# Second block's input projection in seven half-size products, with the gates ahead of attention and the conv projection inside it

## The reference, cut to what matters

```
h   = modulate(rmsnorm(x, norm1_g), shift, scale)            # 1024 x 1024
q, k, v, u, gate_b, gate_c, g_attn, g_conv = split(h @ w_in)  # 1024, 256, 256, 5 x 1024 columns
q, k = axial rope(q), axial rope(k)                           # x * cos + rotate_half(x) * sin
o  = window attention(q, k, v, k_ctx, v_ctx, sink)            # 16 heads, 4 kv heads, +-128 keys + 256 context keys
z  = gate_c * u
y  = gate_b * (w0 * z[t-1] + w1 * z[t] + w2 * z[t+1])         # short conv along the tokens
m  = sigmoid(g_attn) * (o @ w_proj_attn) + sigmoid(g_conv) * (y @ w_proj_conv)
x  = x + mod * (m @ w_out)
```

## Time and profile before

| what | value |
|---|---|
| median of 3 runs | 2936.88 us (2932.27 to 2942.73) |
| the profiled execution | 2934.08 us, its span 2932.3 us |
| PE busy | 96% of the span, DVE 62%, ACT 45%, POOL 18% |
| second block's modulation and first products | about 1165 to 1232 us of the span |
| q and conv groups | to 1581 us |
| attention with the gates | 1582 to 2010 us |
| the two projections | 2011 to 2188 us |

### The profile page before, as it was taken

The page is one execution under the profiler, slowest core; times in us unless marked ns, Lnnn a source line. Parts: engine busy times, 40 slices in busy tenths (PEclk is TensorE's granted clock), DMA queues, the critical chain, the costliest instruction groups (busy, mean ns, idle before and its releaser), DMA issues.

```text
span 2932.3 us, 34943 instructions
## 1 busy us (share of the span) xinstructions
PE 2803.8 (96%) x13928; PEld 2237.2 (76%) x13928; DVE 1827.3 (62%) x2535; ACT 1332.1 (45%) x1927; POOL 527.8 (18%) x437
## 2 busy tenths in 40 slices
PE   8999999999999999999999999999999399999996
PEld 6777777888778778888887666667888378888885
DVE  5344535888875778643223555554445679999997
ACT  4344433333333454211113666664223267777775
POOL 0001202555554011330000111111000300000000
PEclk9999999999999999999999999999999699999998
DMA  4110132445653993411211111115324579999996
GB/s 155 40 44 30 44 108 80 122 134 149 185 151 134 346 265 115 130 44 55 75 51 40 44 41 43 36 41 170 112 92 163 227 282 391 395 398 398 397 394 236
DMA packets 256550, 465.79 MB, mean 159 GB/s; under 512 B 28860, under 2 KB 135508, under 8 KB 255876
## 3 DMA queue, kind: packets, MB, share of 16 engines
q1 hardware_dynamic: 229648, 377.00, 36.8%
q0 software_dynamic: 26592, 86.51, 9.3%
q10 hardware_dynamic: 148, 0.04, 0.0%
HBM read 409.92 MB, written 53.58 MB: 158 GB/s over the span
## 4 chain that ended last, share of the span: by engine, by line
PE 89%; DVE 5%; DMA 2%; ACT 2%; issue 1%; SPq 0%; POOL 0%; POOLq 0%; DVEq 0%; ACTq 0%
PE PS L129 83%; PE PS L132 6%; DVE m L138 2%; DMA m<-in_w_down_dram 1%; ACT m L135 1%; DVE m L144 1%; DVE m L180 0%; DVE m L183 0%; ACT L135 0%; DVE m L177 0%; SPq L186 0%; DMA m<-h_scratch 0%; DVE m L147 0%; DMA m<-in_x_dram 0%; DMA m<-xh_scratch,small 0%
## 5 line engine op out<-in xcount | busy, mean ns | idle before, releaser
L129 PE MATMUL PS<-m,m 128*128 128x512 f32 (+5 forms) x12118 | 2622.8, 389 | 35.2 <-DVE m L138 20.9
L129 PEld LDWEIGHTS PS<-m,m 128*128 128x128 f32 (+2 forms) x12118 | 2034.3, 184 | 548.2 <-issue 115.6
L135 ACT ACTIVATE m<-m 128x512 fp32r<-128x512 f32 (+5 forms) x722 | 735.7, 1040 | 815.0 <-PE PS L129 422.6
L138 DVE TENSOR_TENSOR m<-m,m 128x512 fp32r<-128x512 f32 (+7 forms) x713 | 911.3, 1308 | 251.1 <-ACT m L135 211.7
L135 ACT ACTIVATE m<-PS 128x512 f32<-128x512 f32 (+3 forms) x499 | 280.9, 583 | 497.5 <-PE PS L129 334.4
L138 DVE TENSOR_TENSOR m<-PS,m 128x512 fp32r<-128x512 f32 (+1 forms) x356 | 232.8, 684 | 331.8 <-PE PS L129 297.7
L138 POOL TENSOR_TENSOR m<-m,m 128x512 f32<-128x512 f32 (+3 forms) x166 | 265.0, 1599 | 563.8 <-DVE small L147 207.9
L132 PE MATMUL PS<-ident,m 128*128 128x128 f32 x1586 | 222.9, 280 | 69.1 <-DVE m L153 36.0
L132 PEld LDWEIGHTS PS<-ident,m 128*128 128x128 f32 x1586 | 193.5, 145 | 103.9 <-DVE m L153 36.3
L135 ACT ACTIVATE m<-m,small 128x640 f32<-128x640 f32 (+4 forms) x200 | 157.4, 789 | 220.5 <-DVE small L141 155.0
L147 DVE CUSTOM_DVE_ANT_0 m<-PS,m 128x640 f32<-128x640 f32 (+4 forms) x192 | 146.4, 775 | 118.4 <-PE PS L129 118.4
(11 more groups left out here) (87 smaller groups left out, 489.8 us busy)
## 6 DMA issues: line engine op xcount, KB each, us to landing
m<-in_w_exp_gate_dram SPq DMA_DIRECT2D x64, 1024.0 KB, 8.8
m<-in_w_exp_up_dram SPq DMA_DIRECT2D x64, 1024.0 KB, 9.0
m<-in_w_exp_down_dram SPq DMA_DIRECT2D x64, 1024.0 KB, 8.4
m<-in_w_mod_dram SPq DMA_DIRECT2D x48, 512.0 KB, 3.7
m<-in_w_gate_up_dram SPq DMA_DIRECT2D x44, 512.0 KB, 6.5
m<-in_w_in_dram SPq DMA_DIRECT2D x41, 512.0 KB, 4.1
m<-in_w_in_dram SPq DMA_DIRECT2D x12, 1024.0 KB, 5.2
h_scratch<-m POOLq DMA_DIRECT2D x22, 512.0 KB, 3.5
```

Source lines behind the costliest of these rows:

```text
L129: return Unsent() if self.e is None else self.e.matmul(o, l, r, start=first, stop=last, **k)
L135: return Unsent() if self.e is None else self.e.activation(o, i, fn, **k)
L138: return Unsent() if self.e is None else self.e.tensor_tensor(o, a, b, op)
```

## The change: what it does

- k, q, gate_b/u/gate_c and both gates (25 slabs of 256 weight columns, `ST`) are made by seven half-size products each, ahead of attention, in one loop over c = 0 to 24. v and the context's k, v stay as they were.
- The modulated x2 is kept in place (x2 is stored to DRAM first, tile by tile), and four block differences T1 to T4 are turned and split beside the four plain blocks.
- Rope works on the four quarters of each slab in three buffers, and its results go to DRAM (`q_scratch`); q and k are loaded back before attention.
- The final norm's product on the x2 residual moves from eight instructions in a row to two a pass in four gate passes, with a load and a store of each tile.
- In attention the filler is the conv projection, 16 groups (6 matmuls a step, from step 3 on, three parts after the last step), ended by a product with the loaded gate on DVE (`pc_take`) and a store. The first six steps also split y. The sigmoids and their loads of activation tables leave attention.
- The proj stage has 16 groups in place of 32.

```
+        ST = [("k", 0)] + [("q", c) for c in range(4)] + [
+            p for j in range(4) for p in (("b", j), ("u", 2 * j), ("u", 2 * j + 1))] + [("g", j) for j in range(8)]
+        ST_ORDER = "P1 P6 P2 P7 P5 P4 P3".split()
+        def st_first(act, c):
+            act.wait_ge("st_acc", c, "P1")
+            if c:
+                act.wait_ge("st_up", c - 1, "12")
+            act.activation(su2, ps("st_acc", c, "P1"), ACT.Copy)
...
+        def second_pe(pe):   # the end of it
+            st_product(pe, 0, "P1"), (pe, 0, "P2"), (pe, 0, "P5")
+            4 turns of T2; P7; 4 turns of T4; P6, P4, P3
+            for c in range(1, NST):
+                for P in ST_ORDER:
+                    st_product(pe, c, P)
...
+        def second_dve(dve):  # its loop
+            for c in range(NST):
+                if c == C_AT["b", 0]:
+                    dve.wait_ge("rope_st0", 18)
+                    dve.memset(zb, 0.0)
+                st_u2(dve, c)
+                rope_join(dve, 4 * c - 1)
+                st_low(dve, c + 1, "P1"); st_low(dve, c + 1, "P6")
+                # taps 0 and 1 of the conv tile of pass c - 1, if any
+                st_low(dve, c + 1, "P2")
+                # gate passes 1 to 4: two tiles of residual_norm
+                st_u3(dve, c)
+                rope_turn(dve, 4 * c)
+                # taps 2 and 3
+                st_low(dve, c + 1, "P7")
+                st_c22(dve, c)
+                rope_join(dve, 4 * c); rope_turn(dve, 4 * c + 1)
+                st_low(dve, c + 1, "P5")
+                st_c21(dve, c)
+                rope_join(dve, 4 * c + 1); rope_turn(dve, 4 * c + 2)
+                st_low(dve, c + 1, "P4")
+                st_c12(dve, c)
+                rope_turn(dve, 4 * c + 3); rope_join(dve, 4 * c + 2)
+                st_low(dve, c + 1, "P3")
...
+        def second_pool(pool):  # its loop
+            for c in range(NST):
+                st_sums(pool, c + 1)
+                rope_pool(4 * c - 1); rope_store(4 * c - 2)      # while there is rope
+                rope_pool(4 * c);     rope_store(4 * c - 1)
+                rope_pool(4 * c + 1); rope_store(4 * c)
+                rope_pool(4 * c + 2); rope_store(4 * c + 1)
+                # conv_store, zb_gate (gate_c * u), gate_store, residual_store in their passes
...
+        def rope_join(dve, n):
+            dve.wait_ge("rope_cos", n)
+            dve.wait_ge("rope_sin", n)
+            dve.tensor_tensor(a, a, b_, ALU.add)
...
-                if s == 0:
-                    gate_part(pe, s, 0, 4)
                 if s + 1 < NS2:
                     qk2(pe, s + 1)
-                if s > 1:
-                    gate_part(pe, s, 0, 2)
+                fill_part(pe, s - FILL0, 0)
                 turn2(pe, s, 0)
                 turn2(pe, s, 1)
-                if s > 1:
-                    gate_part(pe, s, 2, 1)
+                fill_part(pe, s - FILL0, 1)
                 if len(chunks2(s)) == 3:
                     turn2(pe, s, 2)
...
+        def mix_dve(dve):   # its first steps
+            for s in range(NS2):
+                if s == 0:
+                    w_low(dve, W_PC)
+                    w_low(dve, W_PC + 1)
                 if s + 1 < NS2:
                     max2(dve, s + 1)
                 p2_evacuate(dve, s, 1)
                 p2_evacuate(dve, s, 2)
+                for h, k in y_parts(s):      # 4 in steps 0 and 1, 2 in steps 2 to 5
+                    y_low(dve, h, k)
...
         def proj_dve(dve):
+            dve.wait_ge("pc_st0")
+            dve.wait_ge("pc_st1")
```

More of the change, by code:

```diff
@@ L332, in program @@
                 pair(w2, 1536 + mt * 128, 3584 + mt * 128)
-        W_G = len(WT)
-        for j in range(16):
-            feat(w2, 4608 + 128 * j, 128)
+        for j in range(8):
+            feat(w2, 4608 + 256 * j)
+        W_PC = len(WT)
+        for j in range(8):
+            feat(w_proj_conv_2[0], 128 * j, 128)
         W_PA = len(WT)
@@ new lines, in st_high @@
+        def st_high(act, c, P):
+            if c == NST:
+                return
+            act.wait_ge(f"w_raw{(W_ST + c) % 2}", W_ST + c)
+            if P in ST_SUM:
+                act.wait_ge("st_sum", c, ST_SUM[P])
+            if c:
+                act.wait_ge("st_acc", c - 1, P)
+            else:
+                act.wait_ge(*w_done.get(W_K2 if ST_PLACE[P] >= 32 else W_V2, ("w_low", 0)))
+            act.activation(st_split(P)[0], st_source(c, P), ACT.Copy).then_inc(*act.did("w_high", W_ST + c, P))
@@ new lines, in st_product @@
+        def st_product(pe, c, P):
+            H, L = st_split(P)
+            Bh, Bl = XB[ST_B[P]]
+            if P == "P2":
+                bank_of["st_acc", c, P] = bank_of["st_acc", c, "P1"]
+                pe.wait_ge("st_s1", c)
+            elif P == "P3":
+                bank_of["st_acc", c, P] = bank_of["st_acc", c, "P5"]
+                pe.wait_ge("st_up", c, "22")
+            else:
+                bank_of["st_acc", c, P] = pe.bank(*{"P1": ("st_c11", c), "P6": ("st_up", c, "U2"), "P7": ("st_up", c, "U3"),
+                                                    "P5": ("st_up", c, "12"), "P4": ("st_up", c, "21")}[P])
+            pe.wait_ge("w_low", W_ST + c, P)
+            st_block_ready(pe, P)
+            for k in range(4):
+                t = mm3(pe, ps("st_acc", c, P), (H[:, k, :], L[:, k, :]), (Bh[:, k, :], Bl[:, k, :]),
+                        k == 0 and P not in ("P2", "P3"), k == 3, **(dict(skip_group_check=True) if P in ("P2", "P3") else {}))
+            t.then_inc(*pe.did("st_acc", c, P))
@@ L2387, in second_act @@
-            md_highs(act, "x", 3, hxh)
+            md_highs(act, 2)
+            md_highs(act, 3)
+            for i in (0, 1):
+                tn_high(act, "T1", i)
+            v2_evacuate(act, 2)
+            for i in (2, 3):
+                tn_high(act, "T1", i)
+            for i in (0, 1):
+                tn_high(act, "T3", i)
+            v2_evacuate(act, 4)
+            for i in (2, 3):
+                tn_high(act, "T3", i)
+            for P in "P7 P6 P4 P3".split():
+                st_high(act, 0, P)
@@ L2400, in second_dve @@
+            act.activation(tab, one, ACT.Exp).then_inc(*act.did("act_table"))
         def second_dve(dve):
             dn_result(dve, "C12")
+            for i in (0, 1):
+                h2_sum(dve, 1, i)
             w_low(dve, W_V2)
+            for i in (2, 3):
+                h2_sum(dve, 1, i)
+            h2_mean(dve, 0)
             modulate_dve(dve, 7)
+            h2_inverse(dve, 0)
+            modulate_dve(dve, 0)
             dve.wait_ge("kc_acc", 1)
             dve.tensor_copy(kc[:, 1, :], ps("kc_acc", 1)[:, 0:256]).then_inc(*dve.did("kc_out_v"))
-            md_lows(dve, "x", 4, hxh, hxl)
@@ new lines, in second_dve @@
+            for i in (6, 7, 0):
+                md_lows(dve, i)
+            tn_diff_dve(dve, 0)
+            v2_evacuate(dve, 7)
+            md_lows(dve, 1)
+            tn_diff_dve(dve, 1)
+            md_lows(dve, 2)
+            tn_diff_dve(dve, 2)
+            md_lows(dve, 3)
+            tn_diff_dve(dve, 3)
+            v2_evacuate(dve, 9)
+            for i in (0, 1):
+                tn_low(dve, "T1", i)
+            for P in "P1 P2 P5".split():
+                st_low(dve, 0, P)
+            for i in (2, 3):
+                tn_low(dve, "T1", i)
@@ L2679, in mix_pe @@
                     values2(pe, s // 4)
+            for p in range(NS2 - FILL0, NFILL):
+                fill_part(pe, p, 0)
+                fill_part(pe, p, 1)
             sums2(pe, 15)
```

994 lines of the change are left out of this document (612 added, 382 removed), and 14 rows, old and new, of the table SHARED.

## The result

The changed kernel takes 2948.4 us (median of 7 runs, 2944.3 to 2952.1), the kernel before 2936.9 beside it (2932.3 to 2942.7); the ratio is 1.0038, with an interval of 1.0026 to 1.0049. I had forecast 2911, range 2883 to 2942: wrong in sign and outside the range. The profiled execution is 2949.8, its span 2948.0.

A forecast was written before the change was run, and what follows sets the result against it. The prediction took PE instructions plus PE's waits to bound the kernel. Its terms, -60.5 + 23.5 + 3 - 1 + 10 + 1 - 1.5 = -25.5 us, gave a median of 2911 us, 8-in-10 range 2883 to 2942.

The forecast's parts named there:

- PE work, -60.5: Whole change: PE's added products and turns less the removed groups, attention filler and half of proj, -60.5 us.
- Attention, steady steps 0: Attention's steady steps: four take 21.4 us, 5.36 a step, with no added PE wait, 0 us.
- Is the loop of a step shorter?: Check in attention that waits for maxima and second exp fit within a step's PE work, the first by 0.6 us.
- a step of attention doesn't shorten: Rival, chance 0.12: next scores wait for DVE's maxima; from 0.53 us a step not faster, at 0.9 2969 us.
- steps over 5.9: Sign that the forecast is wrong: attention steps take over 5.9 us, where 5.4 was expected.
- Transition, -1 (ends -3 and +8): Transition into pass 0: PE's waits, about 4.8 us before, change by -1 us, ends -3 and +8.
- The end of +8: Upper end for the transition into pass 0: each POOL addition of 2.4 us on the way to a turn uncovered.
- Rope, +23.5: Rope passes c = 0 to 4 and their ends: PE waits add 23.5 us, ends +3 and +45.
- the loop through sums and sin: Rope passes: POOL's sums ahead of sin, DVE's join waiting for sin; loop of 22.7 us against a pass of 19.1.
- Start of attention, +10: First attention steps without filler: 15.4 us idle plus 3 of slow clock, against 8 before; +10, ends +3 and +17.
- End of attention, proj, conv and gate passes: After the last step +1 us, the wait before the conv projection's first group -1.5, conv and gate passes +3.
- The ends: Low and high limits given for single terms; for the whole, 2880 (-57) to 2950 (+13) us.

The follow-up runs named there:

- e_actorder: Changed kernel with ACT's evacuation of turn chunk 0 of step s ahead of the first exp of step s+1: 2930.2 us, ratio 0.9973 to the kernel before.
- e_sums0: Changed kernel with POOL's four weight sums for pass 0 behind its five modulation additions, not ahead: 2943.6 us, ratio 1.0016 to the kernel before.
- e_mod_dve: Changed kernel with POOL's pass 0 sums listed behind the modulation and five tiles' modulation additions moved from POOL to DVE: 2948.2 us, ratio 1.0038.
- e_ropepool: Changed kernel with POOL's sin product and store ahead of the next pass's four weight sums in each pass: 2947.2 us, ratio 1.0026.
- e_sin_dve: Changed kernel with rope's product by sin made on DVE behind the product by cos, not on POOL: 2947.9 us, ratio 1.0037.
- e_no_sin: Changed kernel without rope's product by sin on any engine: 2931.4 us in one run.

## Why the prediction was wrong, point by point

- **PE work, -60.5: right as work.** Passes without rope run at 19.26 us, proj fell by 87.7 against 88.7. In attention the work left too, but the time didn't follow it.
- **Attention, steady steps 0: wrong, and the largest error.** "Is the loop of a step shorter?" was asked for two loops (`qk2` behind the maxima, the second exp ahead of its turn) and not for a third, in which the maximum, the exp and the copy of chunk 0 come one after the other ahead of the third turn, which stands ahead of the next scores. Four steps took 23.47 us, not 21.4, and 12 groups x 2.06 = 25 us, against 25.4 missed in this stretch. Of it 16 to 17 are ACT's order (e_actorder); the rest are 0.7 a group of waits for DVE's copies. My rival "a step of attention doesn't shorten" had the place and the cause (filler no longer covers), with the maxima as its mechanism, which isn't the one found. By its kind it is what happened, if smaller: 0.51 us a step over 48 steps, 25 us, where I had said that 34 make the change not faster. I gave it 0.12, since I had checked its margin on one engine's list. My sign of being wrong, "steps over 5.9", was too wide: they took 5.87.
- **Transition, -1 (ends -3 and +8): wrong, inside its ends.** It was +3.3. The sums of pass 0, which I priced at nothing there, cost 5.9 (e_sums0), and without them the transition is 1.6 us shorter than forecast. The end of +8 was made for additions alone, without the sums; moving these to DVE changed nothing (e_mod_dve).
- **Rope, +23.5: 4.9 low, and wrong in its reason.** By the prediction's own 19.1 a pass it was 28.4: 6.5 in pass 0 (3.2 forecast), where PE waits 0.69 for ACT's copy of P1, which the sum doesn't have, and 4.91 for DVE ahead of P3; and 21.9 in passes 1 to 5 (20.3 forecast). A pass took 22.97 against 22.7, but the loop through sums and sin was one way to order the waits; with it undone the time stayed (e_ropepool). The bound is DVE's list plus POOL's hold on it (e_sin_dve, e_no_sin). The agreement of the 22.7 was luck.
- **Start of attention, +10: about right.** The first filler came 26.1 us after the last product against 23.5, with the clock at 0.50 for three windows of 5 us.
- **End of attention, proj, conv and gate passes: right** to 1 or 2 us.
- **The ends.** Those of the single terms add up to -59 and +20, not to the -57 and +13 that the sum states.
- **Outside the sum:** 8.3 us of the profiled spans' difference lie ahead of the change and are mostly the execution's.

With 25.4 for attention, 9.1 for transition and rope, 1.0 for proj and -2.6 for what follows it, -25.5 becomes +7.4. That is what the spans differ by without the first line; what makes it 11.5 in the medians is open.

## What to carry to other kernels

Where filler is taken out of a step, write down each loop from one step's scores to the next, through every engine's list and every bank that two operations of a step share, and compare each with the work that is left; an order that cost nothing under twice the cover may be the new bound, and exchanging two lines may undo it. Count an operation of POOL with two SBUF inputs as DVE's time too, when DVE's list is near full: moving it or its neighbours about changed nothing here, only taking work out did. When a forecast term comes out right, still test its mechanism before building on it.

## What the runs showed of the hardware

- POOL and DVE hold each other up for whole operations with two SBUF inputs: 3.42 us for 1.28 beside an addition of 2.38, and 5.40 for 1.90 through three sums in a row; a DVE addition with a PSUM input kept its 0.68 wholly beside a POOL sum (e_no_sin, at 1295.77). The profile counts the wait as busy time, so DVE's 69% overstates its work.
- TensorE's clock depends on more than the program: a stretch in which PE was busy for the same 17.43 of 20 us was granted 1.00 in one execution and 0.91 in another of the same code, with 113 matmuls done in the one and 102 in the other.
